# Experts of a two-layer decoder: two PSUM banks in turn for gather steps and transposed h, one bank for y in two halves

## The reference

```python
hid = silu(einsum("nd,edf->nef", xn, w1)) * einsum("nd,edf->nef", xn, w3)
hid = hid * combine[:, :, None]        # combine: two of 32 experts per token, the rest zero
y = einsum("nef,efd->nd", hid, w2)
return x + y
```

## Time and profile before

| | |
|---|---|
| median of 3 runs | 1051.97 us (1048.31 to 1052.38) |
| profiled execution, its own time | 1053.49 us |
| its span, first to last instruction | 1051.4 us |
| PE busy | 960.9 us (91%) |
| DVE, ACT busy | 481.1, 470.6 us |
| bytes moved by DMA | 293.37 MB, mean 279 GB/s |
| experts of layer 1, of layer 2 in the span | about 315 to 524 us, 837 to 1043 us |

### The profile page before, as it was taken

One profiled execution on the slowest core, in us unless ns is written; L12 is line 12 of the kernel. 1 busy time (PEld: TensorE's weight loads), 2 busy tenths in 40 slices (PEclk: granted clock), 3 DMA queues, 4 the chain that ended last, 5 costly groups with the idle time before them and its releaser, 6 DMA issues. The chain is left out here.

```text
span 1051.4 us, 19348 instructions
## 1 busy us (share of the span) xinstructions
PE 960.9 (91%) x7942; PEld 778.8 (74%) x7942; DVE 481.1 (46%) x809; ACT 470.6 (45%) x723; POOL 21.9 (2%) x39
## 2 busy tenths in 40 slices
PE   5999999999988999897779999999999889898974
PEld 5898899899885555564478988998998755565542
DVE  5446775567752213121254557655587522121112
ACT  6455555565443333322354555565655433333211
POOL 1010100000000000000000101000000000000000
PEclk9999999999999999999889999999999999999998
DMA  8634544556887999999945345545668789999994
GB/s 282 233 131 160 167 161 161 201 194 227 333 328 286 417 420 420 420 420 421 359 130 199 118 161 167 168 153 201 241 208 359 289 321 419 422 420 420 420 420 187
DMA packets 85480, 293.37 MB, mean 279 GB/s; under 512 B 16976, under 2 KB 17040, under 8 KB 60816
## 3 DMA queue, kind: packets, MB, share of 16 engines
q1 hardware_dynamic: 85392, 292.12, 72.5%
HBM read 291.05 MB, written 1.05 MB: 278 GB/s over the span
## 5 line engine op out<-in xcount | busy, mean ns | idle before, releaser
L1127 ACT ACTIVATE w_high<-weight_ring 128x1024 fp32r<-128x1024 f32 x168 | 176.7, 1059 | 209.1 <-PE ps_a L700 150.4
L1405 DVE TENSOR_TENSOR w_low<-weight_ring,w_high 128x1024 fp32r<-128x1024 f32 x168 | 202.8, 1225 | 139.6 <-ACT w_high L1127 138.9
L698 PE MATMUL ps_a<-xnT_high,w_high 128*128 128x256 f32 x704 | 202.4, 287 | 3.9 <-DVE xnT_low L1411 3.9
L700 PE MATMUL ps_a<-xnT_high,w_low 128*128 128x256 f32 x704 | 199.9, 284 | 0.0
L699 PE MATMUL ps_a<-xnT_low,w_high 128*128 128x256 f32 x704 | 199.3, 283 | 0.0
L698 PEld LDWEIGHTS ps_a<-xnT_high,w_high 128*128 128x128 f32 x704 | 133.9, 190 | 6.6 <-DVE xnT_low L1411 4.7
L699 PEld LDWEIGHTS ps_a<-xnT_low,w_high 128*128 128x128 f32 x704 | 134.5, 191 | 0.5 <-issue 0.5
L700 PEld LDWEIGHTS ps_a<-xnT_high,w_low 128*128 128x128 f32 x704 | 133.4, 190 | 0.0
L1781 DVE TENSOR_TENSOR y_lo<-ps_b,y_hi 128x512 fp32r<-128x512 f32 x64 | 44.3, 692 | 148.3 <-ACT y_hi L1375 145.6
L1095 PEld LDWEIGHTS ps_b<-fold,h 128*128 128x128 f32 x512 | 68.7, 199 | 33.8 <-issue 23.8
L1337 ACT ACTIVATE h<-ps_b 128x512 f32<-128x512 f32 x64 | 38.3, 598 | 114.6 <-PE ps_b L1018 114.6
(11 more groups left out here) (334 smaller groups left out, 1574.9 us busy)
## 6 DMA issues: line engine op xcount, KB each, us to landing
weight_ring<-in_w_in_dram SPq DMA_DIRECT2D x64, 1024.0 KB, 5.1
units_over_splits<-in_w_dram SPq DMA_DIRECT2D x60, 1024.0 KB, 15.9
units_over_attention<-in_w_dram SPq DMA_DIRECT2D x46, 1024.0 KB, 12.5
weight_ring<-in_w_dram SPq DMA_DIRECT2D x40, 1024.0 KB, 15.4
units_over_branches<-in_w_dram SPq DMA_DIRECT2D x30, 1024.0 KB, 14.2
weight_ring<-in_w_branch_dram SPq DMA_DIRECT2D x12, 1024.0 KB, 5.2
unit_over_gates<-in_w_dram SPq DMA_DIRECT2D x10, 1024.0 KB, 12.2
weight_ring<-in_w_out_dram SPq DMA_DIRECT2D x8, 1024.0 KB, 5.8
```

Source lines behind the costliest of these rows:

```text
L698: mm(dst, wh, xh, start=row == 0 and s % 2 == 0, stop=False, skip_group_check=True)
L700: last = mm(dst, wl, xh, start=False, stop=row == rows - 1, skip_group_check=True)
L1127: A(mix_buf(whi, i), mix_raw(i), ACT.Copy).then_inc(hi_ready, 1)
L1405: v.tensor_tensor(mix_buf(wlo, i), mix_raw(i), mix_buf(whi, i).bitcast(F32), ALU.subtract).then_inc(lo_ready, 1)
```

## The change

The four banks of `ps_b` get other uses in the experts. `ps_x` becomes two banks, `ps_xs[0]` and `ps_xs[1]`; every gather step and every `hT` takes the one of its number's parity, and there is a semaphore `taken` for each. So a step waits for the reader of the step before last, not of the last one. `ps_y` becomes one bank. `y(p-1)` is now two steps: the first half stands where `y` stood, the second comes after `hT(2p)` and waits until DVE has read the first half out (`ylo_done`). After the last pair the two halves stand next to each other.

```diff
-    ps_h, ps_x, ps_y = t.ps_b[:, 0, :], t.ps_b[:, 1, :], t.ps_b[:, 2:4, :]
+    ps_h, ps_xs, ps_y = t.ps_b[:, 0, :], [t.ps_b[:, 1, :], t.ps_b[:, 2, :]], t.ps_b[:, 3, :]
...
     def outputs(p):
-        steps.append(("y", (p, len(order))))
+        steps.append(("y", (p, len(order), 0)))
...
+    def outputs_second(p):
+        steps.append(("y", (p, len(order) - 2, 1)))
...
         hidden_T(2 * p)
+        if p:
+            outputs_second(p - 1)
         hidden(2 * p + 1)
...
     outputs(PAIRS - 1)
+    outputs_second(PAIRS - 1)
     steps.append(("scatter", PAIRS - 1))
...
+            def outputs(p, n, n2):
+                if n2 == 0:
+                    arrived(pe, n)
+                    arrived(pe, n + 1)
+                    pe.wait_ge(hid_ready, 2 * p + 2)
+                if p or n2:
+                    pe.wait_ge(ylo_done, 2 * p + n2)
+                for e in range(2):
+                    for j in range(2):
+                        c = 2 * e + j
+                        w2 = unit_buf(n + e)[:, j * D + n2 * 512:j * D + (n2 + 1) * 512]
+                        mm(ps_y[c * SLOTS:(c + 1) * SLOTS, :], t.hid[p % 2][:, e, j, :], w2, start=True,
+                           stop=True, skip_group_check=True).then_inc((y_first, unit_used)[n2], 1)
...
                         kind, k = STEPS[i]
-                        if uses:
-                            pe.wait_ge(taken, uses)
+                        ps_x = ps_xs[uses % 2]
+                        if uses > 1:
+                            pe.wait_ge(taken[uses % 2], uses // 2)
...
                     elif what == "y":
-                        p, n = arg
-                        for n2 in range(2):
-                            act.wait_ge(*((y_first, TILES * (p + 1)), (unit_used, used[n]))[n2])
-                            if p:
-                                act.wait_ge(s_done, 2 * (p - 1) + n2 + 1)
-                            A(t.yhi[:, n2 * 512:(n2 + 1) * 512], ps_y[:, n2, :], ACT.Copy).then_inc(yhi_done, 1)
+                        p, n, n2 = arg
+                        act.wait_ge(*((y_first, TILES * (p + 1)), (unit_used, used[n]))[n2])
+                        if p:
+                            act.wait_ge(s_done, 2 * (p - 1) + n2 + 1)
+                        A(t.yhi[:, n2 * 512:(n2 + 1) * 512], ps_y, ACT.Copy).then_inc(yhi_done, 1)
```

More of the change, by code:

```diff
@@ L436, in layer @@
     rows_given, rows_act, rows_dve = S("first_rows_given"), S("first_rows_act"), S("first_rows_dve")
-    first_given, first_taken, given, taken = S("first_given"), S("first_taken"), S("bank_given"), S("bank_taken")
+    first_given, first_taken, given = S("first_given"), S("first_taken"), S("bank_given")
+    taken = [S("even_bank_taken"), S("odd_bank_taken")]
     h_copied, silu_h, hid_ready = S("h_copied"), S("silu_h_done"), S("hid_ready")
@@ L446, in layer @@
     of_a_round = [unit_used, y_first, sel_ready, selw_ready, rows_given, rows_act, rows_dve, first_given, first_taken,
[L447 removed]
+                  given, *taken, h_copied, silu_h, hid_ready, yhi_done, ylo_done, s_done, s_last, x_added, round_over,
                   round_chain, again_chain, *unit_in]
     psP, psA = t.ps_a, t.ps_b
[L451 removed]
+    ps_h, ps_xs, ps_y = t.ps_b[:, 0, :], [t.ps_b[:, 1, :], t.ps_b[:, 2, :]], t.ps_b[:, 3, :]
     logits = [psA[:, tt, 0:NR] for tt in range(NT)]
@@ L512, in layer @@
     turn = {n: i for i, n in enumerate(ring_units)}
-    y_used = [used[n] for what, arg in steps if what == "y" for n in arg[1:]]
+    y_used = [used[arg[1]] for what, arg in steps if what == "y" and arg[2]]
     def mix_raw(i):
@@ L910, in idle_work @@
                 for _ in range(count):
-                    mm(ps_y[:, 0, 0:P], t.ident[:, :], t.ones[:, :], start=True, stop=True)
+                    mm(ps_y[:, 0:P], t.ident[:, :], t.ones[:, :], start=True, stop=True)
             for q in range(2):
@@ L962, in _ @@
             for tt in range(NT):
-                last = mm(ps_x[:, 0:NE], t.ones_bf[:, :], t.A[:, tt, :], start=tt == 0, stop=tt == NT - 1)
+                last = mm(ps_xs[0][:, 0:NE], t.ones_bf[:, :], t.A[:, tt, :], start=tt == 0, stop=tt == NT - 1)
             last.then_inc(most_counted, 1)
@@ L1360, in _ @@
                                     ACT.Copy)
-                        ins.then_inc(taken, 1)
+                        ins.then_inc(taken[uses % 2], 1)
                     elif what == "hT":
@@ L1725, in _ @@
             dve.wait_ge(most_counted, 1)
-            ch.after(v.tensor_reduce(t.most[:, 0:1], ps_x[:, 0:NE], AX.X, ALU.max))
+            ch.after(v.tensor_reduce(t.most[:, 0:1], ps_xs[0][:, 0:NE], AX.X, ALU.max))
             ch.after(v.tensor_scalar(t.most[:, 1:2], t.most[:, 0:1], SLOTS / 2 - 0.5, 1.0 / SLOTS, ALU.add, ALU.mult))
@@ L1766, in _ @@
                         cw = t.cw[e // BATCH % 2][:, e % BATCH * SLOTS:(e % BATCH + 1) * SLOTS]
-                        v.tensor_tensor(t.u[:, :, :], ps_x[:, 2 * SLOTS:4 * SLOTS].rearrange("p (j s) -> p j s", j=2),
-                                        bc(cw, 1, 2), ALU.mult).then_inc(taken, 1)
-                        dve.wait_ge(taken, uses + 1)
+                        v.tensor_tensor(t.u[:, :, :], ps_xs[uses % 2][:, 2 * SLOTS:4 * SLOTS].rearrange(
+                            "p (j s) -> p j s", j=2), bc(cw, 1, 2), ALU.mult).then_inc(taken[uses % 2], 1)
+                        dve.wait_ge(taken[uses % 2], uses // 2 + 1)
                         if p >= 2:
@@ L1776, in _ @@
                     elif what == "y":
[L1777 to L1782, removed]
+                        p, _, n2 = arg
+                        dve.wait_ge(yhi_done, 2 * p + n2 + 1)
+                        c = slice(n2 * 512, (n2 + 1) * 512)
+                        v.tensor_tensor(t.ylo[:, c], ps_y, t.yhi[:, c].bitcast(F32), ALU.subtract).then_inc(ylo_done, 1)
                 for n in range(2):
```

3 lines of the change are left out of this document (1 added, 2 removed).

## The result

| | before | after |
|---|---|---|
| median | 1051.44 us (20 runs, 1048.01 to 1057.78) | 1055.24 us (20 runs, 1050.70 to 1058.33) |
| ratio of after to before | | 1.0029, 95% interval 1.0015 to 1.0042 |
| profiled execution, its own time | 1053.49 us | 1055.43 us |
| its span | 1051.4 us | 1053.7 us |
| mean granted clock | 0.983 | 0.963 |

The kernel became slower by 0.29% (0.15 to 0.42%), some 3.0 us, against a forecast of +2.1 us and a time of 1054.1. This is clear of zero, and smaller than the 0.5% that counts as no change here. The medians themselves lie 3.8 us apart.

The account below looks back on a forecast made before the run. DMA engines were taken to bound the experts; layer 1: -1.0 (stream) + 1.8 (tail) = +0.8, layer 2: -0.5 + 1.8 = +1.3, together +2.1 us, 1054.1 against the 1051.97 median; 8-in-10 range 1048.5 to 1060 us.

Parts of the forecast that it names:

- The bound: Experts of each layer: DMA engines saturated, share 1.01 at 420 GB/s, so most of PE's gain is waited away later.
- Waits that go, and the one that comes: PE's hT and gather waits, 20.3 us, all go; y's second half waits 0.1 us, or 0.7 in pairs without gather.
- What the loads make of it: SP's queue: hidden(4)'s load moves from 862.29 to about 860.9; stream gains 1.0 us a layer, bounds 0 and 1.4.
- the first hole: Empty DMA slices early in each layer's experts, near 850 to 852 us in layer 2 and 328 in layer 1.
- The last pair: y(14) to y(15): layer 2 keeps 0.5 us of the stream's 1.0, bounds 0 and 1.0; layer 1 keeps all 1.0.
- The tail: After the last y of each layer, nothing covers the new wait: 1.8 us more, 7.7 instead of 5.94, bounds 1.3 and 2.2.
- Rival C: Half clock covers last pair and tail: +2.9 us in layer 2, about 1.5 in each tail, 1060 us; chance 14%.
- my case: Whole kernel: the main forecast of 1054.1 us, own range 1050 to 1057.5, chance 78% with D in it.
- A: Rival on PE in the experts: its waits are worth their time, all 20.3 us gone, 1035 us; chance 3%.
- B: Rival on the loads: both holes of each layer close, stream ends 5.2 us earlier, twice, 1045 us; chance 5%.
- the second hole: Empty DMA slices near 860 to 863 us in layer 2 and 338 to 341 in layer 1, before hidden(4)'s load.
- D: Rival on tail and stream: tail only +1.3 us, stream gains whole 1.4 a layer, 1051.8 us; within my case's 78%.

Follow-up runs that it names:

- experiment 3: Kernel before, with SP's loop loading only the first half of each unit into used ring places: 1022.42 us, ratio to before 0.9725.
- Experiment 4: Changed kernel, with SP's loop loading only the first half of each unit into used ring places: 1010.72 us, ratio to before 0.9618.
- experiment 1: Changed kernel, but the second half of y(15) goes to the free odd bank without waiting for DVE's read: 1048.97 us, ratio to before 0.9974.
- experiment 5: Kernel before with its banks, but y in two steps with hT between them and no new wait: 1055.09 us, ratio to before 1.0038.
- experiment 9: Changed kernel plus idle matmuls, 4 before y(15) and 6 between its halves: 1052.2 us, ratio to before 1.0000.
- experiment 2: Kernel before, plus only the wait of y(15)'s second half for DVE's read of the first: 1054.41 us, ratio to before 1.0026.
- experiment 10: Experiment 1 plus idle matmuls, 8 ahead of y(12) to y(14) and 4 ahead of y(15): 1048.98 us, ratio to before 0.9976.
- experiment 7: Changed kernel plus idle matmuls, 8 before y(15) and 12 between its halves: 1054.99 us, ratio to before 1.0028.
- experiment 8: Experiment 1 plus idle matmuls, 20 ahead of y(12) to y(14) and 8 ahead of y(15): 1052.86 us, ratio to before 1.0013.

## Why the prediction was right

*The bound.* Right. The DMA share of 1.01 decides, and 20.3 us of waits less on PE gave no gain. Experiments 3 and 4 show that it is the loads that take it back: 11.7 us appear as soon as they are halved. How it is taken back was only half right. PE's waits for loads were to grow by nearly what was saved; the waits before `y` grew by 3.6 us, and the same matmuls took 12.8 us more at the lower clock.

*Waits that go, and the one that comes.* All of the earlier trace rows went, as said. The new wait was put at 0.7 us in pairs without a gather and 0.1 in others; it is about 0.5 in the former and never shows in the latter. Experiment 4, in which PE seldom waits for loads, has it 14 times: 12 pairs without a gather and two tails of 1.56, (9.4 - 3.1) / 12 = 0.52 us.

*What the loads make of it.* Load of `hidden(4)`: predicted 860.9, measured 860.77. The w2 units of `y(1)`: 866.1 and 865.96. The steps held, but the term that follows from them was sized too small: I had put the stream 1.0 us earlier, with a bound of 1.4, and `y(14)` starts 1.6 us earlier (experiment 1 the same), about as much as the load of `hidden(4)`, 1.5. The w2 units' late freeing costs nothing in after. The prediction also passed over the units of `y(0)`, freed 1.9 us later: they widen the first hole, but their loads are through by about the time that the load of `hidden(4)` starts, and the stream from there on doesn't move. In experiment 5, where the units of `y(1)` come 2.5 us later instead of 0.2, the stream gains nothing from the order.

*The last pair.* I kept half of 1.0 us for layer 2, 0.5; of 1.6 us 0.94 are kept. What is lost here is the clock's: `y(14)`'s second half takes 1.93 us. Where it was not low, in layer 2 of experiment 9, `y(14)` to `y(15)` took 9.92 us, against 10.78 in after.

*The tail.* The mis-sized term. Predicted 7.7 us, 1.8 more, with a bound of 2.2; measured 9.00 in both layers, 3.06 more. The chain of the sum was right: with a full clock it gives 7.55 (experiments 2 and 9). The missing 1.45 us is the half clock: ACT's copy ends its wait 2.08 us after the second half's start instead of 1.21, and the last additions wait for scatters that take 0.63 us each instead of 0.40. The Trainium skill's rule on throttling (TensorE: Matmul & The Clock Gate, section Terms) gives an estimate of 3.4 us for the 6.8 us at 0.50. The rows show 1.45: ACT and DVE, which have part of the chain, do not get slower with it.

*Rival C* named this mechanism with 14%, at 1.5 us a tail, and was right on the tail, but not on the pair at 2.9 us, which in layer 2 cost 0.9. So after is my case with half of C. That the total was near is partly luck: too small a gain of the stream and too small a tail cancel, 2 x (-0.9 + 3.06) = 4.3 us by the terms, where the runs show 3.0, with an interval of 1.6 to 4.4. A part of the difference may be before's own half-clock pair, as in the earlier trace rows, which after has only in part; how often before has it, one profile doesn't show.

*Rivals A, B, D.* A is refuted by experiments 3 and 4 read together with the result. B did not occur: the second hole nearly closed, but the first grew, and the engines still stand still for 3.4 to 3.6 us a layer, 1.6 less than before, about what `y(14)` gained in layer 2. D's tail of +1.3 never showed, in any run.

## What to carry to other kernels

When buffers are split to take waits away, look first at where the last use stands: a wait that is covered in every pass of a loop is bare after it, and this one undid a gain of 0.26%. The last pass often has free buffers that the others don't; giving it its own bank was the whole repair. Count a wait on PE behind the last load twice: once as itself, once for the clock that may fall in it. And where the loads are the bound, look for saved waits in PE's busy time too: here most of them came back as longer matmuls, at a lower mean clock.

## What the runs showed of the hardware

- The granted clock fell from 1.00 to 0.50 in a tail with a wait of 1.03 us, 1.06 us of matmuls and a wait of 1.56 us, in both layers of after, but with almost the same sequence it stayed at 1.00 in layer 2 of experiment 2, and in its layer 1 it fell only during the second half. With these waits filled by about 1.1 and 1.6 us of idle matmuls it stayed at 1.00 in both layers (experiment 9). Each is one execution.
- At half clock each of the two tails was 1.45 us longer, and that showed in the time (experiment 9); a clock of 0.74 instead of 0.83 over 20 us beside saturated loads did not show in it (experiments 1 and 10).
- One idle fp32 matmul of 128 x 128 is two records in the trace and takes 0.24 to 0.29 us at full clock (20 in 4.73, 12 in 2.94, 4 in 1.14). Whoever sizes idle work needs this number first; experiments 7 and 8 were lost to it.
- Splitting `y` into two steps around `hT`, which frees two units 2.5 us later, with the same work and nearly the same waits, cost 0.38% (0.20 to 0.57%) in experiment 5. The rows explain a quarter of it, and whether the rest is the clock is not tested.
